# Diff mixers: scores of a head pair in two fp32r passes over the whole array instead of one row-tiled fp32 matmul per head

## What is computed

```python
qkv = h @ w_qkv                                    # 1024 -> 3 * 1024
q = q.reshape(B, S, DA_HEADS, 2, DA_QK_DIM)        # 8 heads, each a pair j = 0, 1 of width 64
k = k.reshape(B, S, DA_HEADS, 2, DA_QK_DIM)
v = v.reshape(B, S, DA_HEADS, DA_V_DIM)            # width 128
...
s = jnp.einsum('bqhjd,bkhjd->bhjqk', qb, k).astype(jnp.float32) * scale + bias
s = jnp.where(dist >= 0, s, NEG)
p = jax.nn.softmax(s, axis=-1)
a = p[:, :, 0] - lam_full * p[:, :, 1]
return jnp.einsum('bhqk,bkhe->bqhe', a.astype(v.dtype), v)
```

## Time and profile before

| | |
|---|---|
| median of 3 runs | 2694.57 us (2691.31 to 2696.43) |
| span of the profiled execution | 2693.6 us |
| PE busy | 2653.5 us, 99% |
| DVE busy | 1460.7 us, 54% |
| ACT busy | 1122.8 us, 42% |
| POOL busy | 1167.0 us, 43% |
| first diff mixer, from its first scores to the last quantum | 376.4 to about 605 us |
| second | 2099.9 to about 2328 us |

### The profile page before, as it was taken

How to read it: one execution, slowest core, us unless ns; L and a number is a source line. 1 busy time by engine, 2 the same in 40 slices (tenths; PEclk the granted TensorE clock), 3 DMA queues, 4 the chain that set the end, 5 groups by cost and what they waited for, 6 DMA issues and landing times.

```text
span 2693.6 us, 32187 instructions
## 1 busy us (share of the span) xinstructions
PE 2653.5 (99%) x12935; PEld 2126.5 (79%) x12935; DVE 1460.7 (54%) x2615; ACT 1122.8 (42%) x1521; POOL 1167.0 (43%) x880
## 2 busy tenths in 40 slices
PE   8999999999999999999999999999999999999998
PEld 7787677778888877778888876888888777888887
DVE  5888556657554145657554145575522565575522
ACT  4544544444333236653333236443333344443332
POOL 3454443335445532335445541354455332454453
PEclk9999999999999999999999999999999999999999
DMA  4224032222223221112223331222233222222232
GB/s 164 79 94 172 1 133 86 70 73 96 106 96 110 104 88 63 63 65 98 104 94 110 109 110 48 79 94 98 106 109 110 94 87 71 94 94 94 94 122 81
DMA packets 46597, 253.44 MB, mean 94 GB/s; under 512 B 4528, under 2 KB 11200, under 8 KB 18928
## 3 DMA queue, kind: packets, MB, share of 16 engines
q1 hardware_dynamic: 35376, 231.92, 24.3%
q10 hardware_dynamic: 11072, 19.47, 2.2%
HBM read 249.21 MB, written 10.55 MB: 96 GB/s over the span
## 4 chain that ended last, share of the span: by engine, by line
PE 92%; DVE 4%; ACT 2%; POOL 1%; issue 1%; DMA 0%; SPq 0%; DVEq 0%; ACTq 0%
PE ring L481 79%; PE ring L978 3%; PE turn L983 2%; PE turn L481 1%; PE out L1022 1%; POOL wlo L1219 1%; PE ring L776 1%; PE ring L645 1%; PE out L792 1%; DVE sp L2238 1%; PE out L1028 0%; DVE e L2206 0%; PE out L1110 0%; ACT whi L1270 0%; DVE z L2241 0%
## 5 line engine op out<-in xcount | busy, mean ns | idle before, releaser
L1219 POOL TENSOR_TENSOR wlo<-raw,whi 128x512 fp32r<-128x512 f32 x840 | 1121.8, 1367 | 1456.9 <-ACT whi L1270 1456.8
L481 PE MATMUL ring<-xh,whi 128*128 128x512 f32 x1888 | 753.4, 399 | 9.3 <-DVE xl L1753 8.4
L481 PE MATMUL ring<-xh,wlo 128*128 128x512 f32 x1888 | 736.6, 390 | 0.0
L481 PE MATMUL ring<-xl,whi 128*128 128x512 f32 x1888 | 736.5, 390 | 0.0
L1270 ACT ACTIVATE whi<-raw 128x2048 fp32r<-128x2048 f32 x215 | 411.3, 1914 | 437.1 <-DMA raw<-in_pieces 421.8
L481 PEld LDWEIGHTS ring<-xh,whi 128*128 128x128 f32 x1888 | 354.9, 188 | 114.9 <-issue 41.1
L481 PEld LDWEIGHTS ring<-xh,wlo 128*128 128x128 f32 x1888 | 354.9, 188 | 75.3
L481 PEld LDWEIGHTS ring<-xl,whi 128*128 128x128 f32 x1888 | 355.2, 188 | 72.3 <-issue 3.4
L2391 DVE SCALAR_TENSOR_TENSOR taps<-u,conv,taps 128x511 f32<-128x511 f32 (+1 forms) x344 | 295.7, 905 | 17.3 <-ACT taps L1695 14.8
L2405 DVE TENSOR_TENSOR u<-ring,r 128x512 f32<-128x512 f32 x168 | 114.4, 687 | 299.7 <-PE ring L481 299.7
L481 PE MATMUL ring<-hh,whi 128*128 128x512 f32 (+1 forms) x693 | 265.3, 383 | 0.0
(11 more groups left out here) (304 smaller groups left out, 3423.0 us busy)
## 6 DMA issues: line engine op xcount, KB each, us to landing
raw<-in_pieces SPq DMA_DIRECT2D x215, 1024.0 KB, 4.8
toep<-diag_store ACTq DMA_DIRECT2D x16, 512.0 KB, 3.6
diag_store<-diag_row ACTq DMA_DIRECT2D x1, 5120.0 KB, 25.6
band_store<-band_row ACTq DMA_DIRECT2D x1, 3072.0 KB, 33.1
h<-in_x SPq DMA_DIRECT2D x4, 512.0 KB, 6.3
wbias<-band_store ACTq DMA_DIRECT2D x4, 512.0 KB, 7.2
raw<-in_pieces SPq DMA_DIRECT2D x4, 256.0 KB, 6.4
result<-h SPq DMA_DIRECT2D x2, 512.0 KB, 3.0
```

The source lines that it names most:

```text
L481: ins = pe.matmul(out, stationary, moving, start=first and n == 0, stop=last and n == 2)
L1219: ins = pool.tensor_tensor(m.wlo[slot][:, part], m.raw[slot][:, part], m.whi[slot][:, part].bitcast(F32), ALU.subtract)
```

## The change

Queries and keys of a tile are split as the weights are. `q_s[:, j]` stacks for head j the high part of the queries in one half of the partitions and the low part in the other; `k_hi[:, j]` holds the high keys of head j in both halves; `k_lo[j]` holds its low keys in one half and zeros in the other. Two fp32r passes over all 128 partitions then give high by high plus low by high, and high by low. Queries and keys now have one buffer each (`q_d`, `k_d`), and the second `e` tile one buffer for both parities.

```diff
-STARTS = {"diff": (24, 47, 70, 92, 115, 139, 163, 184), "stick": ...
+STARTS = {"diff": (26, 48, 72, 94, 118, 141, 166, 185), "stick": ...
...
+    def stacked_pair(b, t, i, n):
+        for j in range(2):
...
+            out, queries = m.ring[2 + j][:, 0:n], m.q_s[:, j, i * P:(i + 1) * P]
+            pe.matmul(out, queries, m.k_hi[:, j, 0:n], start=True, stop=False)
+            pe.matmul(out, queries, m.k_lo[j][:, 0:n], start=False, stop=True).then_inc(m["su_ready"], 1)
...
-            pe.wait_ge(m["pu_taken"], b.at("pu_taken", K_UNIT[t] + 1))
+            pe.wait_ge(m["q_low"], b.at("q_low", 2 * t + 2))
+            pe.wait_ge(m["k_high"], b.at("k_high", 4 * t + 4))
+            pe.wait_ge(m["k_low"], b.at("k_low", 2 * t + 2))
             for i in range(TT):
-                score_pair(b, t, i, m.qt[t % 2], m.kt[t % 2], 0, CAUSAL_W[i])
+                stacked_pair(b, t, i, CAUSAL_W[i])
...
+    def queries_high(b, t):
+        act.wait_ge(m["pu_taken"], b.at("pu_taken", K_UNIT[t]))
+        for j in range(2):
+            act.activation(m.q_s[half_of(j), j, :], m.q_d[half_of(j), :], ACT.Copy).then_inc(m["q_high"], 1)
+    def keys_high(b, t):
+        act.wait_ge(m["pu_taken"], b.at("pu_taken", K_UNIT[t] + 1))
+        for j in range(2):
+            act.activation(m.k_hi[half_of(j), j, :], m.k_d[half_of(j), :], ACT.Copy).then_inc(m["k_high"], 1)
+        for j in range(2):
+            act.activation(m.k_hi[half_of(1 - j), j, :], m.k_d[half_of(j), :], ACT.Copy).then_inc(m["k_high"], 1)
...
+            if t % 2 == 0 and t + 1 < TILES:
+                queries_high(b, t + 1)
             hi_at(b, "diff", t, 1)
...
+            if t % 2 and t + 1 < TILES:
+                queries_high(b, t + 1)
             hi_at(b, "diff", t, 2)
+            if t + 1 < TILES:
+                keys_high(b, t + 1)
...
+    def queries_low(b, t):
+        dve.wait_ge(m["q_high"], b.at("q_high", 2 * t + 2))
+        for j in range(2):
+            dve.tensor_tensor(m.q_s[half_of(1 - j), j, :], m.q_d[half_of(j), :],
+                              m.q_s[half_of(j), j, :].bitcast(F32), ALU.subtract).then_inc(m["q_low"], 1)
+    def keys_low(b, t):
+        for j in range(2):
+            dve.wait_ge(m["k_high"], b.at("k_high", 4 * t + 1 + j))
+            dve.tensor_tensor(m.k_lo[j][half_of(j), :], m.k_d[half_of(j), :],
+                              m.k_hi[half_of(j), j, :].bitcast(F32), ALU.subtract).then_inc(m["k_low"], 1)
...
+        for j in range(2):
+            chain(dve.memset(m.k_lo[j][half_of(1 - j), :].bitcast(F32), 0.0))
```

More of the change, by code:

```diff
@@ L165 @@
 SUMS_AHEAD = 2
-STARTS = {"diff": (24, 47, 70, 92, 115, 139, 163, 184), "stick": (24, 46, 68, 91, 115, 139, 163, 181),
+STARTS = {"diff": (26, 48, 72, 94, 118, 141, 166, 185), "stick": (24, 46, 68, 91, 115, 139, 163, 181),
           "window": (30, 44, 60, 68, 76, 84, 92, 100)}
@@ L200, in mix @@
         if mixer == "diff":
+            t.update(q_high=16, q_low=16, k_high=32, k_low=16)
             t.update(exped=64, rl_ready=8, c1_ready=8, e1_scaled=32, normed=32, o_taken=8, osq_ready=8, osum_done=8,
@@ L279, in vector_pieces, with half_of @@
     return [b.at("piece", 3) for name, b in stages.items() if name.startswith("w_o")]
+def half_of(j):
+    return slice(64 * j, 64 * j + 64)
 def project_bank(m, unit):
@@ L415, in __init__ @@
         self.v = [self.at(f"v{i}", [P, TT, 256], o + 40960 + 4096 * i) for i in range(2)]
-        self.e = [[self.at(f"e{i}{j}", [P, PACKED], o + 49152 + 10240 * i + 5120 * j) for j in range(2)]
-                  for i in range(2)]
+        e_1 = self.at("e1", [P, PACKED], o + 59392)
+        self.e = [[self.at(f"e{i}0", [P, PACKED], o + 49152 + 5120 * i), e_1] for i in range(2)]
+        self.q_d = self.at("q_d", [P, S], o + 32768)
+        self.k_d = self.at("k_d", [P, S], o + 34816)
+        self.q_s = self.at("q_s", [P, 2, S], o + 36864, F32R)
+        self.k_hi = self.at("k_hi", [P, 2, S], o + 65536, F32R)
+        self.k_lo = [self.at(f"k_lo{j}", [P, S], o + 14336 + 16384 * j, F32R) for j in range(2)]
         self.aT = [self.at(f"aT{i}", [P, PACKED], o + 69632 + 5120 * i) for i in range(2)]
@@ L979, in score_pair @@
                       start=True, stop=True).then_inc(m["su_ready"], 1)
+    def stacked_pair(b, t, i, n):
+        for j in range(2):
+            u = 8 * t + 2 * i + j
+            if u < 2:
+                pe.wait_ge(m["unit_taken"], b.at("unit_taken", 0))
+            else:
+                pe.wait_ge(m["su_taken"], b.at("su_taken", u - 1))
+            out, queries = m.ring[2 + j][:, 0:n], m.q_s[:, j, i * P:(i + 1) * P]
+            pe.matmul(out, queries, m.k_hi[:, j, 0:n], start=True, stop=False)
+            pe.matmul(out, queries, m.k_lo[j][:, 0:n], start=False, stop=True).then_inc(m["su_ready"], 1)
     def turn_blocks(src, places):
@@ L2157, in take_qk_v, with take_diff @@
             take_feature(b, unit, m.kt[n // 2], 1.0)
+    def take_diff(b, unit):
+        g, n = divmod(unit, 6)
+        if n == 4 and g == 0:
+            take_rtok(b)
+        if n >= 4:
+            take_v(b, unit, m.v[g % 2], n - 4)
+        elif n % 2 == 0:
+            take_feature(b, unit, m.q_d, -0.125)
+        else:
+            take_feature(b, unit, m.k_d, 1.0)
+    def queries_low(b, t):
[8 more added lines that the diff above has]
+                              m.k_hi[half_of(j), j, :].bitcast(F32), ALU.subtract).then_inc(m["k_low"], 1)
     def mix_diff(b, layer):
@@ L2207, in mix_diff @@
                                              block(t, 1, i), ALU.mult, ALU.add).then_inc(m["normed"], 1)
+                if t % 2 and t + 1 < TILES:
+                    take_diff(b, 3 * t + 4)
+                    queries_low(b, t + 1)
+                elif t + 1 < TILES:
+                    keys_low(b, t + 1)
             if 1 <= t < TILES + 1:
@@ L2217, in mix_diff @@
                                          m.ov[h % 2][:], ALU.mult, ALU.mult).then_inc(m["on_ready"], 1)
-            if t < TILES - 2:
-                take_qk_v(b, 3 * t + 4, -0.125)
+            if t % 2 == 0 and t < TILES - 2:
+                take_diff(b, 3 * t + 4)
     def take_low(b, t):
```

17 lines of the change are left out of this document (12 added, 5 removed).

## The result

The changed kernel takes **2719.59 us** (median of 4 runs, 2717.06 to 2721.20), the kernel before 2694.57 us in the same comparison (median of 3 runs; a fourth took 9223.89 us, far off all others, and is not counted): ratio 1.0092, interval 1.0079 to 1.0104. It is slower, by 25 us, where 2704 us was forecast with a range of 2687 to 2712. The direction was right, the size was not.

What follows compares the result with a forecast made beforehand. PE's order of matmuls was taken as the bound, DVE's loop as second. Losses 16.5 less gains 11.7 us a mixer make 9.6 for two; on the 2693.6 us span that gives 2703.2, as median 2704, range 2687 to 2712.

Steps and rivals of the forecast that it cites:

- Score matmuls: PE's score pairs: a tile costs 2.52 us instead of 3.79, a gain of 10.0 us a mixer.
- Rivals 3 and 4: Fp32r at 128 columns costs as fp32, 2708 to 2710, chance 0.11; the 0.41 stays with every score group, 2730, 0.02.
- `pv` behind v: For odd tiles `pv` waits for v behind the reads; one read now runs ahead, gaining 1.1 us a mixer.
- start (first and second pair): Tile 0's first scores wait for query and key preparation, the second pair for reads behind later bias loads: 3.2 us lost.
- tile 0 (turn, then low keys): POOL's split slows low query and combination before the turn, then two low keys before the next scores: 3.7 us lost.
- tile 2, bank of the keys: PE needs tile 3's keys taken at 16.5 us into tile 2, but DVE finishes at 17.6: 1.1 us lost.
- turn 6: Tile 6's turn waits for the combination behind two low queries, with only 19 quanta to the next start: 2.9 us lost.
- reads of tiles 3, 5, 7: PE's second pairs wait for first reads, queued on DVE behind combination and low keys: 0.8, 1.1, 0.7 us lost.
- keys of tiles 2, 4, 6: Scores of even tiles wait for low keys prepared in the tile before, low queries under POOL: 0.4, 1.0, 0.7 us lost.
- end (early output): Mixer's end: one quantum fewer before the last low tile's use, and a later v take: 0.9 us lost.
- Rivals 1 and 2: ACT and DVE finish before PE except start and end, 2679.5 us, 0.11; POOL's split misses low parts, 2695, 0.26.
- DVE's loop is the second bound: Inside a diff mixer DVE's loop of reads, scaling, combination and keys is nearly as long as PE's tile.

Runs made afterwards that it cites:

- row_split: Changed kernel with scores from three fp32r passes of 64 rows, row-tiled, in place of stacking; one 128-row copy and low part each for queries and keys: 2703.9 us.
- kept_busy: Changed kernel with filling matmuls on PE ahead of the scores of tiles 0 and 1 and ahead of turn 6, both diff mixers: 2713.2 us.
- prep_once: Changed kernel without the rounded copies and low parts of queries and keys for tiles 1 to 7 of both diff mixers: 2687.9 us.
- lows_once: Changed kernel without DVE's low parts of queries and keys for tiles 1 to 7 of both diff mixers, ACT's copies kept: 2690.2 us.
- whole_lows_at: lows_last_at with the keys' low parts in one subtraction over 128 rows, no zeros, and ACT's copies adapted: 2695.3 us.
- whole_keys_first: whole_lows_at with odd tiles' keys rounded ahead of ACT's split, low keys sooner on DVE, and filling matmuls at the window mixer's start: 2691.7 us.
- early_zeros: Changed kernel with zero fills ahead of the norm and bias transfers of tiles 0 and 1 ahead of the first rounded queries: 2717.8 us.
- lows_last_at: early_zeros with odd tiles' low queries behind the combination on DVE and, on even tiles, ACT's split ahead of the rounded queries: 2715.0 us.

## Why the prediction was wrong in size

**Score matmuls: right.** PE's timeline at pairs of 128 and of 512 keys in the changed kernel:

```profile
450.31 0.22 PE L1003 MATMUL ring<-k_hi,q_s 128*128 128x128 f32 x1
450.37 0.28 PE L1004 MATMUL ring<-k_lo,q_s 128*128 128x128 f32 x1
450.48 0.27 PE L1003 MATMUL ring<-k_hi,q_s 128*128 128x128 f32 x1
450.59 0.27 PE L1004 MATMUL ring<-k_lo,q_s 128*128 128x128 f32 x1
...
457.00 0.39 PE L493 MATMUL ring<-xh,wlo 128*128 128x512 f32 x1
457.23 0.40 PE L1003 MATMUL ring<-k_hi,q_s 128*128 128x512 f32 x1
...
458.60 0.39 PE L493 MATMUL ring<-xh,wlo 128*128 128x512 f32 x1
```

A pass of 128 columns takes 0.11 us, and 458.60 - 457.00 less three steps is 0.92. A tile costs 2.56 us for the forecast 2.52. Rivals 3 and 4 fall. The rule of the Trainium skill on row tiles (TensorE: Matmul & The Clock Gate, section "Measured speedup vs the span model") fails here again: row_split shows 0.5 us beyond the columns, not some 4 ns. **`pv` behind v:** idle time fell from 3.0 to 1.7 us, 0.65 a mixer where 1.1 was counted.

**Losses**, in the first mixer, us beyond each group's own price:

| step | forecast | measured |
|---|---|---|
| start (first and second pair) | 3.2 | 4.65 |
| tile 0 (turn, then low keys) | 3.7 | 0.8 + 2.1 |
| tile 2, bank of the keys | 1.1 | 1.4 |
| turn 6 | 2.9 | 4.0 |
| reads of tiles 3, 5, 7 | 0.8, 1.1, 0.7 | 1.1, 1.3, 0 |
| keys of tiles 2, 4, 6 | 0.4, 1.0, 0.7 | 0.9, 1.7, 1.0 |
| turn 4 | 0 | 0.55 |
| end (early output) | 0.9 | 0.8 |

The measured ones sum to 20.3 against 16.5; less gains of 11.05 (9.8, 0.65 and 0.6) that is 9.25 of the 10.7 us, and the other 1.4 are quanta at the slow clock. So every place but turn 4 was named, and tile 0 and the reads were even counted a little high. (The start's 4.65 are 3.35 of wait and 1.30 of slow quanta ahead of the second pair; most of the last 1.4 follow turn 6.) The forecast's sign, PE idle for some 16 us a mixer, came out at 15.9 us as the profile counts idle time, though the mixer lost more than was forecast. Start, turn 6 and the keys of even tiles came out 4.1 us higher, partly by the clock, partly by small terms: the queries' take began 1.34 us behind the norm, not 1.0 (two fills, with 0.17 of idle time ahead of each), ACT's copies of 64x512 come every 0.65 us, not every 0.55, and on even tiles the split behind two such copies moved POOL further over the scaling (4.33 us in tile 6 where 3.29 was counted). The low parts themselves were right, 1.40 us for two and 3.45 under POOL ahead of tile 1 (forecast 3.4); one over 128 rows follows its predecessor by 0.60 in row_split, so what the Trainium skill says (VectorE: DVE Perf Modes, section "Two Vector instructions with no wait between them") agrees, with 0.1 us for each.

**The step that failed** is the price of a wait: the forecast read the granted clock as full in all slices, kept it so for the changed kernel, and priced each wait at its own length, with no term for the clock behind it. In the changed kernel the waits bring the clock to its lower level, and the quanta behind them take 0.43 us a pass. kept_busy puts this at 7.4 us for the two mixers. For the two mixers the forecast was 24.2 - 9.6 = 14.6 us short; 7.4 is the clock. The rest, 7.2 us, is waits that were sized too small: at full clock a mixer loses 8.4 us (254.0 - 245.6), where 4.8 was forecast. The terms are those above, start, turn 6 and the keys of even tiles.

**Rivals 1 and 2** (the cover holds; half the collisions) were the wrong way to doubt: prep_once and lows_once show a gain only with the preparations gone, and then 3.1 and 1.6 us in the first mixer, where rival 1 had 7.6 with them in place. That DVE's loop is the second bound was right: lows_once.

Not settled: why the clock fell more in the second mixer than in the first at waits of the same length. Nor why it stayed up behind the 1.7 us ahead of the first scores in whole_lows_at and fell behind as long a wait in whole_keys_first; 1.9 us there were followed by a fall in early_zeros and by none in lows_last_at. Not every execution of one kernel need fall alike.

## What to carry to other kernels

Moving work from a full PE to a half busy DVE pays only where the new work does not lie in the loop that PE closes with it; price each tile's chain through DVE, ACT and POOL against PE's tile, not the mean share. Where PE was busy without a break, a new wait of 2 to 3 us can cost well more than its length (here 2.3 and 5.1 us on top of the 5.7 us of the two longest waits of a mixer), and independent matmuls can fill it. If operands need preparing, count instructions over full 128 rows: one in place of two was worth more here than any change of order. It was to be had because the scores may also get a low by low term of the other half.
